# Alternating the two heads of a pair in the score and value products of a windowed attention on TensorE

## What is computed

```python
q = partial_rope(rmsnorm(q, q_gain), positions)      # 256 x 16 x 64
k = partial_rope(rmsnorm(k, k_gain), positions)      # 256 x  2 x 64
# for each block i of 128 queries, keys of block i-1 and i
s = einsum('bqkgd,bskd->bkgqs', qb, kb) * scale
s = where(valid, s, -inf)                             # band and causal
p = softmax(concatenate([s, sink_col], -1))[..., :-1]
o = einsum('bkgqs,bskd->bqkgd', p, vb)
x = x + g1 * (o @ w_o)
```

## Time and profile before

| | |
|---|---|
| Median of 3 runs | 1078.32 us (1077.26 to 1079.16) |
| Profiled execution | 1075.63 us |
| Its span | 1073.8 us |
| TensorE busy | 1006.7 us, 94% of the span |
| VectorE busy | 785.3 us, 73% |
| ScalarE busy | 505.1 us, 47% |
| Mean granted TensorE clock | 0.948 of full speed |

### The profile page before, as it was taken

How to read it: one execution, slowest core, us unless ns; L and a number is a source line. 1 busy time by engine, 2 the same in 40 slices (tenths; PEclk the granted TensorE clock), 3 DMA queues, 4 the chain that set the end, 5 groups by cost and what they waited for, 6 DMA issues and landing times.

```text
span 1073.8 us, 19690 instructions
## 1 busy us (share of the span) xinstructions
PE 1006.7 (94%) x7559; PEld 955.1 (89%) x7559; DVE 785.3 (73%) x1108; ACT 505.1 (47%) x773; POOL 32.5 (3%) x48
## 2 busy tenths in 40 slices
PE   3699889999999999999999999999998999999997
PEld 2696669999999988977899999998887989999997
DVE  6885884898869877675489876987874679876432
ACT  3334753554334454535454443345956554443433
POOL 4000000000000000000100000002000000000000
PEclk9997759899999989999989999998999889999998
DMA  8980458499748968263159974899403439974510
GB/s 301 366 299 15 135 188 266 160 361 327 256 157 315 345 233 312 79 235 119 53 171 361 317 261 159 315 342 302 171 1 96 142 95 363 351 247 156 198 38 40
DMA packets 144414, 232.17 MB, mean 216 GB/s; under 512 B 6250, under 2 KB 75410, under 8 KB 144354
## 3 DMA queue, kind: packets, MB, share of 16 engines
q1 hardware_dynamic: 142993, 228.75, 61.4%
q0 software_dynamic: 1072, 2.05, 0.9%
q10 hardware_dynamic: 288, 0.54, 0.2%
HBM read 230.27 MB, written 1.05 MB: 215 GB/s over the span
## 4 chain that ended last, share of the span: by engine, by line
PE 83%; DVE 8%; ACT 4%; issue 3%; DMA 1%; SPq 0%; DVEq 0%; ACTq 0%
PE M L1440 21%; PE M L1442 21%; PE M L1441 21%; DVE ACC L952 3%; PE AUX L1940 3%; DVE WL L929 2%; PE M L1458 2%; PE M L1460 2%; DMA RAW<-in_ada_w 1%; PE M L1464 1%; ACT WH L581 1%; PE AUX L1784 1%; PE AUX L1565 1%; PE M L1728 1%; PE M L1727 1%
## 5 line engine op out<-in xcount | busy, mean ns | idle before, releaser
L1440 PE MATMUL M<-XH,WH 128*128 128x256 f32 x1424 | 408.5, 287 | 3.5 <-DVE XL L1016 2.3
L1441 PE MATMUL M<-XL,WH 128*128 128x256 f32 x1424 | 404.7, 284 | 0.0
L1442 PE MATMUL M<-XH,WL 128*128 128x256 f32 x1424 | 404.6, 284 | 0.0
L929 DVE TENSOR_TENSOR WL<-RAW,WH 128x2048 fp32r<-128x2048 f32 x136 | 309.3, 2290 | 84.8 <-ACT WH L581 84.7
L581 ACT ACTIVATE WH<-RAW 128x2048 fp32r<-128x2048 f32 x136 | 258.4, 1912 | 233.5 <-PE M L1442 146.7
L1440 PEld LDWEIGHTS M<-XH,WH 128*128 128x128 f32 x1424 | 275.2, 193 | 5.6 <-issue 3.6
L1441 PEld LDWEIGHTS M<-XL,WH 128*128 128x128 f32 x1424 | 275.3, 193 | 0.2
L1442 PEld LDWEIGHTS M<-XH,WL 128*128 128x128 f32 x1424 | 275.1, 193 | 0.0
L952 DVE SCALAR_TENSOR_TENSOR ACC<-ADA,COND,ACC 128x512 f32<-128x512 f32 x266 | 199.8, 751 | 9.5 <-DMA ADA<-in_ada_w 0.3
L1440 PE MATMUL M<-MH,WH 128*128 (+1 forms) x528 | 149.1, 282 | 0.6 <-DVE TMP L1031 0.6
L1441 PE MATMUL M<-ML,WH 128*128 (+1 forms) x528 | 148.6, 281 | 0.0
(11 more groups left out here) (246 smaller groups left out, 1153.8 us busy)
## 6 DMA issues: line engine op xcount, KB each, us to landing
ADA<-in_ada_w SPq DMA_DIRECT2D x68, 1024.0 KB, 6.2
RAW<-in_w_gate SPq DMA_DIRECT2D x44, 512.0 KB, 6.3
RAW<-in_w_up SPq DMA_DIRECT2D x44, 512.0 KB, 7.8
RAW<-in_w_down SPq DMA_DIRECT2D x44, 512.0 KB, 6.1
RAW<-in_w_ffn_in SPq DMA_DIRECT2D x44, 512.0 KB, 5.9
RAW<-in_wqkv_b SPq DMA_DIRECT2D x24, 512.0 KB, 6.1
RAW<-in_w_ffn_out SPq DMA_DIRECT2D x22, 512.0 KB, 4.2
RAW<-in_w_in SPq DMA_DIRECT2D x16, 512.0 KB, 7.6
```

Of the source, the lines that this page charges most:

```text
L929: dve.tensor_tensor(WL[:, s, :], RAW[:, s, :], WH[:, s, :], ALU.subtract).then_inc(l_ready, 1)
L1440: pe.matmul(out_ap, wh, xh, start=start, stop=False, skip_group_check=True)
L1441: pe.matmul(out_ap, wh, xl, start=False, stop=False, skip_group_check=True)
L1442: return pe.matmul(out_ap, wl, xh, start=False, stop=stop, skip_group_check=True)
```

## The change

In sa_scores the six products of a pair are put in the order: first product of head 0, of head 1, second product of head 0, of head 1, mask of head 0, of head 1. In sa_rows the same is done with the three value products, and TensorE waits for the copies of both heads before the first of them, where it waited for each head's copy before that head's products. The instructions, their operands and their number are the same.

```diff
             def sa_scores(b):
 
+                pair = []
                 for e in range(2):
                     rows = slice(HD * e, HD * e + HD)
                     keys = QA[rows, 8, :] if e == b // 4 else KS[rows, :]
-                    bank = MB[:, 2 - 2 * (b % 2) + e, :]
+                    pair.append((MB[:, 2 - 2 * (b % 2) + e, :], rows, keys))
+                for bank, rows, keys in pair:
                     pe.matmul(bank[:, 0:P], QA[rows, b, 0:P], keys[:, 0:P], start=True, stop=False, skip_group_check=True)
+                for bank, rows, keys in pair:
                     pe.matmul(bank[:, P:3 * P], QA[rows, b, P:2 * P], keys, start=False, stop=False, skip_group_check=True)
+                for bank, rows, keys in pair:
                     mm = pe.matmul(bank[:, 0:3 * P], IDB[:, :], MASKA[:, :], start=False, stop=True, skip_group_check=True)
                 mm.then_inc(sa_s, 1)
...
                 if b >= 1:
                     pe.wait_ge(xin_ready, KT + b)
+                pe.wait_ge(sa_ptc, 2 * b + 2)
+                outs = [AUX[HD * e:HD * e + HD, 4, :] for e in range(2)]
                 for e in range(2):
-                    pe.wait_ge(sa_ptc, 2 * b + e + 1)
-                    rows = slice(HD * e, HD * e + HD)
-                    o = AUX[rows, 4, :]
-                    pe.matmul(o[:, 0:P], VA[:, 0, kv], PT[:, b % 2, e, 0:P], start=True, stop=True, skip_group_check=True)
-                    pe.matmul(o[:, P:2 * P], VA[:, 0, kv], PT[:, b % 2, e, P:2 * P], start=True, stop=False, skip_group_check=True)
-                    mm = pe.matmul(o[:, P:2 * P], VA[:, 1, kv], PT[:, b % 2, e, 2 * P:3 * P], start=False, stop=True, skip_group_check=True)
+                    pe.matmul(outs[e][:, 0:P], VA[:, 0, kv], PT[:, b % 2, e, 0:P], start=True, stop=True, skip_group_check=True)
+                for e in range(2):
+                    pe.matmul(outs[e][:, P:2 * P], VA[:, 0, kv], PT[:, b % 2, e, P:2 * P], start=True, stop=False, skip_group_check=True)
+                for e in range(2):
+                    mm = pe.matmul(outs[e][:, P:2 * P], VA[:, 1, kv], PT[:, b % 2, e, 2 * P:3 * P], start=False, stop=True,
+                                   skip_group_check=True)
                 mm.then_inc(sa_o, 1)
```

## The result

The changed kernel took 1071.96 us, median of 5 runs (1069.36 to 1072.34), beside 1077.26 for the kernel before (1076.93 to 1079.16). The ratio is 0.9938, 95% interval 0.9922 to 0.9955: 6.7 us less, between 4.9 and 8.4. The profiled execution took 1069.36 us with a span of 1067.6, where that of before had 1075.63 and 1073.8.

What follows compares the result with a forecast made beforehand. TensorE was taken as the bound outside the attention, with TensorE and DVE waiting on each other inside it; 2.77 us (through pair 3) plus 3.16 (pairs 5 and 7) gave 5.9 off 1078.32, so 1072.4 us, range 1070.9 to 1077.0.

Steps and rivals of the forecast that it cites:

- part 3: Sum of gains along the attention's path: 2.77 us at pair 3 plus 3.16 for pairs 5 and 7, 5.9 us.
- the clock term: Attention: the clock may rise less with TensorE less busy; path scores already costed at the low level, so no cost.
- The pair of scores: Attention: a pair of scores takes 2.4 us in place of 4.0 at 1.2 GHz, 1.6 us saved.
- Scores 0 and 1: Start of the attention: DVE's maximum of pair 0 starts 0.33 us earlier, that of pair 1 1.94 us earlier.
- Pair 3: Attention: scores 3 end at 108.9 at the low clock; their maximum starts at 108.95 in place of 111.72, 2.77 us gained.
- Pairs 5 and 7: Later attention: DVE waits 1.65 us for each pair's scores; 1.58 us of each goes through, 3.16 us together.
- The value products: Attention: alternated, a pair takes 1.55 us for 1.96 at 1.2 GHz; off the path except for pair 0.
- The clock in the projection: Output projection: each microsecond the clock rise shifts moves the end by 0.43 us; 3 us either way is 1.3 us.
- overlap in program order: Rival, scores: head 1's long product starts with head 0's last pass; 4.7 us gained, 1073.6 us; chance 0.22.
- no overlap of row halves: Rival, scores: only the handover goes, 0.35 to 0.41 us a pair; 1.95 us gained, 1076.4 us; chance 0.16.
- Loss behind the attention: Rival, after the attention: later clock rise or colliding loads lose 4 us of 5.9, 1076.5 us; chance 0.10.
- exposed weight loads: Rival, scores: eight loads a pair come into the open, adding 2.0 us; 8 us slower, 1086 us; chance 0.06.

Runs made afterwards that it cites:

- First trace: The changed kernel's profiled execution, nothing further changed: 1069.36 us, attention 64.81 us.
- Second and third: Two later traces of the changed kernel, nothing further changed: attention 64.30 and 64.29 us; the kernel timed again had ratio 0.9915.
- fourth experiment: Changed kernel, but in the scores head 0's two products stand ahead of head 1's two, masks still last: 1069.79 us, ratio 0.9922.
- third experiment: Changed kernel, but head 1's score products read partitions 0 to 63 like head 0's, so both use the same row half: 1074.96 us, ratio 0.9969.
- its kin with short scores: Changed kernel with value products as before (0.9924), with head 0's score products ahead of head 1's (0.9922), or with masks first (0.9924).

## Why the prediction missed in size, and where it was right

The prediction was 1072.4 us, a gain of 5.9; measured were 1071.96 and a ratio that puts the gain at 6.7. The sign, the place and the mechanism were right, and the sizes were too small. The median lies in the range of 1070.9 to 1077.0, but 0.9938 x 1077.26 = 1070.6 lies 0.3 us below it, and so do two of the five runs (1069.36 and 1069.84). That the median came within 0.5 us of the forecast is luck: the sum was too small by about as much as the level that it was taken from was too high.

**The steps that failed** are the sum of part 3, 5.9 us, with the clock term that was put at nothing ("this costs nothing more"), and the level of 1078.32 us. The traces give 6.3, 6.8 and 6.8 us at max 7 in place of 5.9. Step by step, in us, counted from the first score product so that the start drops out (max 1 is VectorE's maximum of pair 1):

| Step | Forecast gain | First trace | Second and third |
|---|---|---|---|
| max 1 | 1.94 | 1.82 | 2.34 |
| max 3 | 2.77 | 2.86 | 3.39 |
| pair 5, further | 1.58 | 1.82 | 1.75 |
| pair 7, further | 1.58 | 1.64 | 1.69 |
| sum, at max 7 | 5.9 | 6.3 | 6.8 |

- **The pair of scores** was right: forecast 2.4 us at 1.2 GHz, measured 2.35. The split of its saving, 0.41 for the handover and 1.18 net for the overlap, came out as 0.41 and 1.26. That the column halves of the value products speak for row halves was right; the lag of 0.1 was 0.01. One head's mask, put at 0.32 us, took about 0.33: two masks take 0.76 us with what follows, one took 0.43.
- **Scores 0 and 1, forecast 0.33 and then 1.61.** In the second and third trace scores 1 start 9.52 us behind scores 0, before it was 10.17: 0.65 earlier, not 0.33. Of this 0.50 comes over VectorE, whose maximum of pair 0 starts 0.43 us earlier and is 0.07 shorter, though its row showed a wait of 0.34 only; the other 0.15 comes from the rotation, of which more was done before the clock fell. The pair itself gives 0.08 more than forecast. In the first trace the clock fell 4.1 us behind the attention's start instead of 5.1, which takes 0.5 back.
- **Pair 3, the clock put at nothing.** I took scores 3 at the low level, done at 108.9, with DVE free at 108.7. In all three traces they ran at 2.4 GHz and DVE did not wait: another 0.2 us. That DVE's list comes next was right.
- **Pairs 5 and 7.** I capped each at ScalarE's idle 1.58 us. VectorE's whole wait of 1.65 went, for pair 5 with 0.10 to 0.17 us more: 3.46 and 3.44 us together in place of 3.16.
- **The clock, then, is a part of the miss and not the whole.** In the second and third trace it gives about 0.15 + 0.2 of the 0.9 us too little; most of the rest is idle time that was worth more than its rows say. The forecast said that with less work on TensorE the clock may rise less; over the attention it was higher, 0.72 and 0.70 where it had been 0.63.
- **The level and the range.** The forecast stood on a median of three runs, 1078.32, where five gave 1077.26, so all of its figures stand 1.06 us too high; from 1077.26 the lower end would have been 1069.8, and 1070.6 would lie above it. That end held only a lag of zero and an early rise in the projection. It left out the clock ahead of the attention, which the change doesn't touch and which moves an execution by about 1.5 us for each low stretch.
- **The value products**: forecast 1.55 us a pair at 1.2 GHz, from the first to what follows; measured 1.48 (pair 0 of the second trace, 103.21 to 104.69) where it was 1.96, and off the path as said. In the earlier trace rows head 1's first product starts ahead of three more passes of head 0, not four: the third stands there at 126.94.
- **The clock in the projection**: earlier in one trace of three, by 1.5 us; at the forecast 0.43 us for each that is 0.65, and about 0.6 was seen. The other two did not change.
- **The rivals**: overlap in program order is refuted by the fourth experiment, no overlap of row halves by the pair's 2.35 us beside 3.61 in the third. As a kernel of its own the third gave 2.16 us in the attention, forecast 1.95, but that is luck: scores 3, forecast 1.25, gave 0.07, and scores 5, forecast 0.35, gave 1.73, since the clock fell otherwise. Loss behind the attention is refuted by the table of traces, exposed weight loads by the pair's length.

What remains open: the ratios of the changed kernel and of its kin with short scores (0.9938, 0.9915, 0.9924, 0.9922, 0.9924) centre near 8 us, while the traces show 6.7 to 7.7 us from the attention's start on. A part of this is known. Of 40 timed executions of before on record, ten took 1079.95 to 1082.57 us, longer than any that was traced (1078.61 at most); of 29 of the changed kernel and its kin none took more than 1072.34. The medians of all 40, 1077.6, and of the changed kernel's eleven, 1069.84, differ by 7.7 us. Where the long executions of before lose their time no trace shows.

## What to carry to other kernels

Two products on different halves of TensorE's rows run side by side if nothing that uses all rows stands between them (here they wrote to different banks; the same bank was not tried for row halves): look for the mask, the transpose or the bias that separates them, and move that, whatever the order of the rest. Before counting on it, ask which engine waits for these products and for how long; here it was 1.65 us of 1.67 saved for two pairs, and nothing for two others. Such an idle row is a little too small as a price: 0.34 us gave 0.43, and 1.65 gave 1.64 to 1.82. And before comparing one trace with another, cut both at the place of the change: the stretch ahead of it, with the same code, differed by up to 3.1 us. And look at the clock inside that place too: in the third experiment a total came out as forecast from two steps that were both wrong.

## What the runs showed of the hardware

- Float32 products of 64 rows overlap fully: two heads' eight passes take 1.59 us to the first mask (134.34 to 135.93), one head's four took 1.58 (122.43 to 124.01); the pair is 1.26 us shorter than one after the other at 1.2 GHz, with a lag of 0.01 us.
- TensorE starts work for a free half ahead of work that stands before it in the program: ahead of three passes of the other half in the scores, with a lag of 0.01 us, and ahead of three in the value products of before, with 0.49 us. The Trainium skill (TensorE: Matmul & The Clock Gate, Part 3) has matmuls start strictly in program order; these traces show otherwise.
- A handover between 64-row products and 128-row ones and back costs 0.41 us at 1.2 GHz, in agreement with the drain that the Trainium skill names (TensorEngine Tiling (Array Packing), Key Properties).
- The granted clock over the attention rose from 0.63 to 0.72 where TensorE's busy time fell from 61.11 of 71.13 us to 45.75 of 64.81; in windows, from 0.50 to 0.67 where it fell from 12.00 of 12 us to 9.62, and from 0.50 to 0.73 where it fell from 12.79 of 15 us to 8.25. In the third experiment TensorE was busy for 24.00 of 24 us at 0.50 throughout. I had expected the opposite, if anything. What raises it was not tried.
